# Layer B of a two-layer decoder: the next group's decay rows, key products and first base steps are made in slots 9 to 15 of the running group

## The reference

```python
conv = silu(causal_conv4(proj));  q, k, v = split(conv)
q = l2norm(q) * SCALE;  k = l2norm(k)
beta = sigmoid(b);  g = -exp(a_log) * softplus(a + dt_bias);  gc = cumsum(g in the chunk)
decay = exp(gc_i - gc_j) for j <= i
lmat = strict_lower(beta * k k^T * decay)
u, w = solve (I + lmat) [v*beta | k*beta*exp(gc)]
aqk = (q k^T) * decay;  kdec = k * exp(g_last - gc)
per chunk: v_new = u - w S;  o = (q exp(gc)) S + aqk v_new;  S = S exp(g_last) + kdec^T v_new
```

## Time and profile before

| what | value |
|---|---|
| median of 3 runs | 2171.14 us (2170.03 to 2179.94) |
| the profiled execution, its own time | 2173.54 us |
| its span, first to last instruction | 2171.6 us |
| mean granted TensorE clock over the span | 0.989 of full |
| busy: PE, DVE, ACT, POOL | 97%, 45%, 32%, 21% |
| layer B's group rounds | about 1117 to 1733 us of the span |

### The profile page before, as it was taken

The page is one execution under the profiler, slowest core; times in us unless marked ns, Lnnn a source line. Parts: engine busy times, 40 slices in busy tenths (PEclk is TensorE's granted clock), DMA queues, the critical chain, the costliest instruction groups (busy, mean ns, idle before and its releaser), DMA issues.

```text
span 2171.6 us, 39599 instructions
## 1 busy us (share of the span) xinstructions
PE 2110.4 (97%) x16046; PEld 1508.9 (69%) x16046; DVE 986.9 (45%) x2521; ACT 688.4 (32%) x1615; POOL 450.8 (21%) x640
## 2 busy tenths in 40 slices
PE   8999999999999999999999999999998999999998
PEld 6888888888888876554566666666666666665444
DVE  5244354354344444321256666666666233333252
ACT  4122321312222131311145454444544344542101
POOL 0512231242124205000033312332231200020000
PEclk9999999999999999999999999999998999999999
DMA  7412201212221156777012212221110262124451
GB/s 234 151 41 67 81 26 46 78 40 56 74 59 42 30 183 226 228 220 219 23 57 92 75 74 86 74 85 76 59 42 13 62 269 82 39 74 140 135 167 53
DMA packets 210250, 210.53 MB, mean 97 GB/s; under 512 B 14262, under 2 KB 181654, under 8 KB 209151
## 3 DMA queue, kind: packets, MB, share of 16 engines
q1 hardware_dynamic: 198070, 148.27, 23.0%
q0 software_dynamic: 12000, 59.73, 7.1%
HBM read 179.56 MB, written 68.23 MB: 114 GB/s over the span
## 4 chain that ended last, share of the span: by engine, by line
PE 47%; DVE 3%; ACT 1%; issue 0%; DVEq 0%
PE bank L2093 17%; PE bank L2857 8%; PE bank L3347 7%; PE bank L2151 4%; PE bank L2167 2%; PE bank L2149 2%; DVE arena L2591 1%; PE bank L2159 1%; PE bank L2873 1%; PE bank L2882 1%; PE bank L3325 1%; PE bank L3358 0%; PE bank L2182 0%; PE bank L3254 0%; PE bank L3231 0%; ACT L2354 0%
## 5 line engine op out<-in xcount | busy, mean ns | idle before, releaser
L887 PE MATMUL bank<-arena 128*128 128x256 f32 (+1 forms) x2688 | 631.7, 386 | 0.0
L887 PEld LDWEIGHTS bank<-arena 128*128 128x128 f32 x2688 | 494.5, 190 | 75.3
L2093 PE MATMUL bank<-arena 128*128 128x352 f32 x1296 | 462.9, 474 | 0.1
L2093 PEld LDWEIGHTS bank<-arena 128*128 128x128 f32 x1296 | 219.8, 193 | 65.3 <-issue 0.6
L2857 PE MATMUL bank<-arena 128*128 128x352 f32 x576 | 176.4, 459 | 0.0
L3347 PE MATMUL bank<-arena 128*128 128x512 f32 x360 | 167.5, 599 | 0.0
L2151 PEld LDWEIGHTS bank<-arena 128*128 128x128 f32 x864 | 128.8, 196 | 42.9 <-DVE arena L2605 5.0
L2857 PEld LDWEIGHTS bank<-arena 128*128 128x128 f32 x576 | 106.6, 190 | 53.3
L2151 PE MATMUL bank<-arena 128*128 128x128 f32 x864 | 133.9, 282 | 3.8 <-DVE arena L2605 3.8
L1341 POOL TENSOR_TENSOR arena<-arena 128x272 f32<-128x272 f32 (+1 forms) x48 | 31.5, 656 | 507.9 <-ACT arena L1061 488.0
L1323 POOL TENSOR_TENSOR arena<-arena 128x512 f32<-128x512 f32 x96 | 122.7, 1278 | 10.9 <-POOL arena L1323 0.9
(11 more groups left out here) (430 smaller groups left out, 2783.7 us busy)
## 6 DMA issues: line engine op xcount, KB each, us to landing
arena<-in_w_in_a SPq DMA_DIRECT2D x48, 512.0 KB, 5.2
arena<-in_w_in_b SPq DMA_DIRECT2D x40, 512.0 KB, 5.1
arena<-in_cache_win_k SPq DMA_DIRECT2D x48, 256.0 KB, 6.2
arena<-in_cache_win_v SPq DMA_DIRECT2D x48, 256.0 KB, 4.7
out<-arena SPq DMA_DIRECT2D x40, 256.0 KB, 3.4
arena<-in_w_mem_kv SPq DMA_DIRECT2D x16, 512.0 KB, 8.1
arena<-in_cache_mem_k SPq DMA_DIRECT2D x32, 256.0 KB, 4.6
arena<-in_cache_mem_v SPq DMA_DIRECT2D x32, 256.0 KB, 3.8
```

The source lines that it names most:

```text
L887: m = nc.tensor.matmul(o[:, 0:hi - lo], w, y, start=k == 0 and i in (0, 1, 3, 5), stop=k == KH - 1, skip_group_check=i in (2, 4, 6))
L2093: m = nc.tensor.matmul(bank[j % 3][:, 0:PART], ring.slots[:, (B1 + b) % RING, k, :], part_in(k, part_), start=k == 0, stop=k == KD - 1)
```

## The change

Rows rl, their exponentials, kk, the choice of 8x8 blocks, the base rows and the first two base steps of group G+1 are made in slots 9 to 15 of round G, into a second buffer (`LTs`). ra and qk of group G move to slots 9 and 11, kt to 6, vt to 15. The levels move to slots 4 to 7, 10 and 12 to 14: level 5's z from slot 13 to 12, level 6's x from 14 to 13, level 3's x from 6 to 4. The exponentials of ra(G) and rl(G+1) come together in ACT's slot 9. The convolution, tap and SiLU tables change; SiLU 0 of group G+2 moves from slot 7 to slot 12, SiLU 1 from 12 to 13, SiLU 2 from 15 to slot 0 of the next round. The output turn moves from slot 9 to 8. The base steps leave out column 0 of their chosen blocks, which no step reads. Ahead of the loop rl, kk and two base steps of group 0 are made. The diff, cut to its core:

```diff
-    picked = upper[:, 0:P].rearrange("p (c j b) -> p c j b", j=BASE, b=NBASE)
+    picked = upper[:, 0:4 * (BASE - 1) * NBASE].rearrange("p (c j b) -> p c j b", c=4, b=NBASE)
-    spread_rows = upper[:, 2176:2176 + 4 * BASE * 32]
+    spread_rows = upper[:, 2176:2176 + 4 * (BASE - 1) * 32]
+    LTs = [LT, upper[:, 3072:3584].rearrange("p (c e) -> p c e", e=P)]
...
-    PREP = {0: ("rl", "ra"), 1: ("kk", "qk"), 10: ("kt",), 11: ("vt",)}
-    LEVEL_SLOTS = {(3, "x"): 6, (3, "z"): 7, (4, "x"): 8, (4, "z"): 9, (5, "x"): 12, (5, "z"): 13, (6, "x"): 14, (6, "z"): 15}
-    BASE_STEPS = {2: 2, 3: 2, 4: 2, 5: 1}
-    BASE_END = max(BASE_STEPS)
-    AT_SS, AT_ROOTS, AT_INV, AT_LOGS, AT_FACTORS, AT_OT = 3, 4, 5, 6, 7, 9
+    PREP = {6: ("kt",), 9: ("ra", "rl"), 11: ("qk", "kk"), 15: ("vt",)}
+    NEXT = ("rl", "kk")
+    LEVEL_SLOTS = {(3, "x"): 4, (3, "z"): 5, (4, "x"): 6, (4, "z"): 7, (5, "x"): 10, (5, "z"): 12, (6, "x"): 13, (6, "z"): 14}
+    AT_ROWS = 13
+    STEPS_BEFORE = {14: 1, 15: 1}
+    STEPS = {0: 1, 1: 2, 2: 1, 3: 1}
+    EARLY_STEPS = sum(STEPS_BEFORE.values())
+    AT_EXPS = 9
+    AT_SS, AT_ROOTS, AT_INV, AT_LOGS, AT_FACTORS, AT_OT = 3, 4, 5, 6, 7, 8
-    def p_names(s):
-        return PREP.get(s, ()) + ((level_name(*level_in[s]),) if s in level_in else ())
+    def p_names(G, s):
+        names = [(G + (n in NEXT), n) for n in PREP.get(s, ())]
+        if s in level_in:
+            names.append((G, level_name(*level_in[s])))
+        return [(g, n) for g, n in names if g < NG_]
...
-    work = [(0, "ss")]
+    work = [(0, "ss"), (0, "rl"), (0, "kk")]
-                work += [(G, n) for n in p_names(s)]
+                work += p_names(G, s)
...
-    TAP_AT = {3: 0, 8: 1, 11: 2}
-    conv_at = {4: (0, 1), 5: (0, 2), 7: (0, 3), 9: (1, 1), 11: (1, 2), 12: (1, 3), 13: (2, 1), 14: (2, 2), 15: (2, 3)}
-    silu_at = {7: 0, 12: 1, 15: 2}
+    TAP_AT = {0: 0, 4: 1, 11: 2}
+    conv_at = {1: (0, 1), 3: (0, 2), 4: (0, 3), 5: (1, 1), 7: (1, 2), 8: (1, 3), 12: (2, 1), 14: (2, 2), 15: (2, 3)}
+    silu_at = {12: 0, 13: 1}
...
-                if c:
-                    readout(pe, g, f"ks{c}")
+                readout(pe, g, f"ks{c}" if c else "vt")
-        def matrix_step(G, s):
+        def turned(G, name):
-            if s == 0:
+            if name == "rl":
+            elif name == "ra":
-            elif s == 1:
+            elif name == "kk":
+            elif name == "qk":
-            if "kt" in PREP.get(s, ()):
+            elif name == "kt":
-            if "vt" in PREP.get(s, ()):
+            elif name == "vt":
+        def matrix_step(G, s):
+            cs, lt = range(*GR[G % 2]), LTs[G % 2]
+            for g, name in p_names(G, s):
+                if name in PREP.get(s, ()):
+                    turned(g, name)
...
-                        to_blocks(G, f"x{k}", [(i, 16 * n, LT[q, n, q], side(Md[q, n, :], k, 0))
+                        to_blocks(G, f"x{k}", [(i, 16 * n, lt[q, n, q], side(Md[q, n, :], k, 0))
...
-        for u in units[NORM_AT:PER_HEAD + AHEAD]:
+        for u in units[NORM_AT:PER_HEAD + KD]:
+            unit(*u)
+        turned(0, "rl")
+        for u in units[PER_HEAD + KD:PER_HEAD + 2 * KD]:
+            unit(*u)
+        turned(0, "kk")
+        for u in units[PER_HEAD + 2 * KD:PER_HEAD + AHEAD]:
...
-        for i in range(3):
-            silu(1, i)
-        for u in ended(units[PER_HEAD:PER_HEAD + AHEAD]):
-            piece(*u)
+        first, second, third = ended(units[PER_HEAD:PER_HEAD + AHEAD])
+        piece(*first)
+        silu(1, 0)
+        exps(0, "rl", LT, 0)
+        piece(*second)
+        silu(1, 1)
+        silu(1, 2)
+        piece(*third)
-                    if s == 0:
-                        exps(G, "rl", LT, 0)
-                    elif s == 1:
+                    if s == AT_EXPS:
+                        if G + 1 < NG_:
+                            exps(G + 1, "rl", LTs[(G + 1) % 2], 0)
...
+                if 0 < G < NG_ - 1 and s == 0:
+                    silu(G + 1, 2)
...
             nc.vector.tensor_scalar(brT[:, g // 2, g % 2 * 512:(g % 2 + 1) * 512], b[:, :], onw, None,
                                     ALU.mult).then_inc(rd_dve, 1)
+        def turned(G, name):
+
+            h, cs = group(G)
+            lt, factors_of = LTs[G % 2], hd[:, h % 2]
+            b = left(dve, G, name)
+            if name == "rl":
+                nc.vector.tensor_tensor(lt, bk(b), wide4(mat(M_GT)), ALU.add).then_inc(rd_dve, 1)
+            elif name == "ra":
+                nc.vector.tensor_tensor(AT[:, cs, :], bk(b), wide4(mat(M_GE)), ALU.add).then_inc(rd_dve, 1)
+            elif name == "kk":
+                dve.wait_ge(exd, 2 * G + 1)
+                nc.vector.tensor_tensor(lt, lt, bk(b), ALU.mult).then_inc(rd_dve, 1)
+            elif name == "qk":
+                dve.wait_ge(exd, 2 * G + 2)
+                nc.vector.tensor_tensor(AT[:, cs, :], AT[:, cs, :], bk(b), ALU.mult).then_inc(rd_dve, 1)
+            elif name == "kt":
+                dve.wait_ge(hdv, 3 * G + 3)
+                nc.vector.tensor_tensor(kdec[:, cs, :], bk(b), factors_of[:, KD_, cs].unsqueeze(2)
+                                        .to_broadcast([P, 4, P]), ALU.mult).then_inc(rd_dve, 1)
+            elif name == "vt":
+                nc.vector.tensor_tensor(vb[:, cs, :], bk(b), hcols(beta, h)[:, cs].unsqueeze(2)
+                                        .to_broadcast([P, 4, P]), ALU.mult).then_inc(rd_dve, 1)
+
+        def choose_blocks(G):
+
+            readout(dve, G, "kk")
+            for i in range(4):
+                q = quarter(i)
+                nc.vector.tensor_tensor(picked[q].rearrange("p c j b -> p c b j"),
+                                        LTs[G % 2][q, :, q].rearrange("p c (b j) -> p c b j", j=BASE)[:, :, :, 1:],
+                                        mats[q, M_HSEL, 4:4 + NBASE].unsqueeze(1).unsqueeze(3)
+                                        .to_broadcast([32, 4, NBASE, BASE - 1]), ALU.mult).then_inc(base, 1)
+
         def matrix_step(G, s):
             h, cs = group(G)
...
+            for g, name in p_names(G, s):
                 if name in PREP.get(s, ()):
...
+                    turned(g, name)
             if s in level_in:
                 k, x = level_in[s]
                 hi = P // 2
...
-                                .to_broadcast([P, 4 * BASE, NBASE, BASE])).then_inc(base, 1)
+                                .to_broadcast([P, 4 * (BASE - 1), NBASE, BASE])).then_inc(base, 1)
-            rows_ = spread_rows.rearrange("p (c j b e) -> p c j b e", c=4, j=BASE, b=NBASE)[:, :, j, :, 0:j]
+            rows_ = spread_rows.rearrange("p (c j b e) -> p c j b e", c=4, b=NBASE, e=BASE)[:, :, j - 1, :, 0:j]
...
+                readout(dve, g, "vt")
...
-        for g in range(2):
-            for i in range(3):
-                for w in range(CW):
-                    conv(g, i, w)
-                if (g, i) == (0, 0):
-                    gate_sums_read()
-                if (g, i) == (0, 2):
-                    norm_inverses(0)
+        for i in range(3):
+            for w in range(CW):
+                conv(0, i, w)
+            if not i:
+                gate_sums_read()
+        norm_inverses(0)
+        for w in range(CW):
+            conv(1, 0, w)
+        turned(0, "rl")
+        for w in range(CW):
+            conv(1, 1, w)
+        turned(0, "kk")
+        choose_blocks(0)
+        for w in range(CW):
+            conv(1, 2, w)
+        base_rows(0)
+        for n in range(EARLY_STEPS):
+            base_step(0, n)
...
-                if G < NG_ and s in BASE_STEPS:
-                    before = sum(n for t, n in BASE_STEPS.items() if t < s)
-                    if not before:
-                        base_rows(G)
-                    for n in range(before, before + BASE_STEPS[s]):
+                if G < NG_ and s in STEPS:
+                    first = EARLY_STEPS + sum(n for t, n in STEPS.items() if t < s)
+                    for n in range(first, first + STEPS[s]):
-                    if s == BASE_END:
+                    if first + STEPS[s] == BASE - 1:
+                if G + 1 < NG_:
+                    if s == AT_ROWS - 2:
+                        choose_blocks(G + 1)
+                    elif s == AT_ROWS:
+                        base_rows(G + 1)
+                    elif s in STEPS_BEFORE:
+                        first = sum(n for t, n in STEPS_BEFORE.items() if t < s)
+                        for n in range(first, first + STEPS_BEFORE[s]):
+                            base_step(G + 1, n)
```

More of the change, by code:

```diff
@@ L2231, in matrix_step @@
                     if k < LEVELS - 2:
-                        to_blocks(G, f"x{k}", [(i, 16 * n, LT[q, n, q], side(Md[q, n, :], k, 0))
+                        to_blocks(G, f"x{k}", [(i, 16 * n, lt[q, n, q], side(Md[q, n, :], k, 0))
                                                for n, i, q, _ in over])
                     elif k < LEVELS - 1:
```

(28 more changed lines are left out.)

## The result

The changed kernel takes 2255.16 us in the median of 4 runs (2251.71 to 2260.40), the kernel before 2171.72 us in the same comparison. The ratio is 1.0378, 95% interval 1.0345 to 1.0412: slower by 3.8%, where 4.4% was forecast, and 13 us under the predicted time. The profiled execution took 2254.04 us, its span is 2252.1.

The account below looks back on a forecast made before the run. PE, busy 97%, was taken as the bound. From 2173.5 us profiled, -24.4 - 4.8 - 15.3 + 79 + 3 + 44 + 13.6 + 1.4 gave 2270.0; less 2.4 to the median, 2268 us, range 2205 to 2310.

Parts of the forecast that it names:

- Base steps ahead: PE's wait for the block transpose before level 3 goes, -24.4 us; other waits from the same crowded slots go, -4.8 us.
- POOL's queue: Late SiLU delays POOL's squares and spread; PE waits 6.1 us at level 6's x, +79 us; round 0 adds 3.
- The table load: On ACT ahead of slot 12's SiLU: 1.28 us by the trace, without the skill page's further 1.38 us drain.
- the rival with a longer switch: ACT drains longer ahead of the SiLU, each wait about 1.28 us longer: 17 us more, 2285 us; chance 0.04.
- Clock: PE's clock loss behind old waits goes, -15.3 us; half clock behind each new wait costs 3.4 us, +44 us.
- Exponentials together: In ACT's slot 9 eight exponentials delay vn's copy; PE waits 0.8 us in 12 rounds, 2 in two: +13.6 us.
- Ahead of the loop: PE's turn of rl(0) waits for DVE's convolution (1, 0), small head terms and factors: +1.4 us.
- The rival on the other side: POOL's spread is in time, so level 6's x doesn't wait and the gain stands: 2142 us; chance 0.08.

Follow-up runs that it names:

- The repaired kernel: The changed kernel with POOL's spread ahead of squares(G+2, 0) and, on ACT, rl(G+1)'s exponentials behind vn's copy: 2145.65 us, ratio 0.9866.
- two moves in the old order: The kernel before with base steps and transpose ahead of DVE's factor work, and convolution steps (0, 1) and (0, 2) one slot later: 2147.76 us, ratio 0.9870.
- the kernel with the steps first: The kernel before with DVE's base steps and block transpose ahead of out_factors, norm_inverses and factors in each slot: 2155.64 us, ratio 0.9905.
- squares twice: The changed kernel with squares(G+2, 0) made twice on POOL, one more operation ahead of the spread: 2281.27 us, ratio 1.0492.

## Why the prediction was right

By its own steps, in its order:

- **Base steps ahead**, -24.4 and -4.8 us: the first is exact, since no wait for the transpose is left. Of the 4.8 us, 1.4 are left for r_sb. The reason given, crowded slots, was not the right one: a change of order in the same slots took 17.7 of the 24.4 us.
- **POOL's queue**, +79 and +3 us: the mechanism is as put, link by link. Counted from PE's start of slot 12 at 1445.76, the copy of qs ends at +2.1 (forecast +2.1), the SiLU at +4.2 (+4.0), the spread at +6.9 (+7.3), DVE's reading at +7.9 (+8.2), and PE starts at +8.0 (+8.3). In a round PE stands 5.7 us and not 6.1. The term that was too large is the spread: 1.63 us for the 2.17 of the earlier trace rows, a round in which POOL's first operation started behind a convolution step of DVE; in nine of the 16 rounds of before the two took 1.7. In round 0 PE's wait is 2.05 us for 3, and in round 13 it is 6.3.
- **The table load**: 1.28 us with the SiLU's first operation 0.01 us behind it, as the earlier trace rows had it, so the rival with a longer switch falls. The 1.38 us of drain that the Trainium skill gives, ScalarE: Activation LUTs, section What ACT_TABLE_LOAD costs, are not in this trace.
- **Clock**: -15.3 and +44, so +28.7 us of PE's time. This is the term that was mis-sized most. In the group rounds the kernel before lost 16.6 us and the changed one 31.9, of which 4.6 in the last rounds and 27.2 around the waits of rounds 1 to 12; over the whole span the difference is 11.7. That the clock falls at each of these waits was right. The step that failed is the price of one, 3.4 us, taken as the middle of two losses and kept though the wait is longer than those before: it is 2.3, because the spell at 1.2 GHz begins while PE still stands.
- **Exponentials together**, +13.6 us: 9.9. In the steady round PE waits 0.4 us and not 0.8; once the long wait was gone, the total was 15.6.
- **Ahead of the loop**, +1.4: 1.2 us.

By the profiled executions the forecast was +96.5 us and the span grew by 80.5, 16 us less. The errors of the terms are -5.2 (82 forecast and 76.8 found for the wait at level 6), -17.0 (clock), -3.7 (vn), -0.2 (ahead of the loop) and +1.4 (r_sb); against them stand the 7.2 us of PE's busy time that are not clock and that no term of the sum had. That is -17.5 in all. So the mechanism was right, and the sum is as near as it is in part by luck: without the 7.2 us it would have been 7 us further off. The ends of the range were not added up rightly either: its own terms give 2196 for the lower (2268 - 44 - 14 - 13.6) and about 2300 for the upper, not 2205 and 2310. The result lies well inside both.

The rival on the other side, a spread in time, had its condition right: once it was in time, the kernel was faster than before, though by 0.5% and not by the 1.4% that it gave. In the profiled executions the gain was 13.0 us and not 29.5. The rival had taken the other waits and the lost clock as gone; the rows show 3.6 us left at level 6's x, 2.7 for r_sb, 2.0 more than its 13.6 for vn, and PE's busy time shorter by 9.3 us and not 15.3. The repaired kernel's 0.9866 is what the rival gave, but by luck: it has hardly a wait for vn, which the rival had counted.

Two things the prediction did not see. It took the change's gain as one that needed the change, where two moves in the old order give the same. And it called the slots of the base steps crowded, where the trace of before already held the better reason: a last step that stood behind work waiting for ACT and also ran at a fifth of its speed.

## What to carry to other kernels

When work moves between slots, look for the engine whose program was not edited: its order still holds the old promise, here that a SiLU comes six slots before its round's spread is wanted. Follow each moved result to everything that waits in the same queue behind its reader, not only to the reader. And before building a second buffer to take work off a path, read the timeline of the last microseconds ahead of the wait: a wait for another engine, or an operation five times its usual length, may be moved away by a change of order alone, as it was here.

## What the runs showed of the hardware

**DVE beside POOL.** In the kernel before, DVE's L2591 with 16 columns took 0.97 us, until POOL's scaling L2761 was over:

```profile
1311.49 1.03 POOL L2761 TENSOR_TENSOR arena<-arena 128x512 f32<-128x512 f32 x1 [3.68 <-DVE arena L2503]
1311.60 0.97 DVE L2591 TENSOR_TENSOR arena<-arena 128x16 f32<-128x16 f32 x1
```

The first ends at 1312.52, the second at 1312.57. The same pair stands in 14 of the 16 rounds, and the step takes 0.96 to 1.03 us in each. In the kernel with the steps first it took 0.19 us in all 16, with no scaling of POOL beside it. It goes the other way too: where POOL's first spread operation starts just behind a convolution step of DVE (L2458), as in the round of the earlier trace rows (1321.51 behind 1321.44) and three others, it takes 1.13 to 1.15 us and not 0.62. The Trainium skill, SBUF — State Buffer, section Who interferes with whom, says that a DVE instruction with two SBUF inputs contends with a GpSimd instruction that reads SBUF. The trace agrees: in these rows the one that starts later is the one that is lengthened, and it ends only after the earlier one has ended.

**A longer wait can cost less clock.** The half-clock spells around the waits at level 6's x, in rounds 1 to 12 of each kernel: waits of 1.2 to 1.3 us (SiLU in slot 10) had none of their own; 3.6 to 3.7 us (late SiLUs in the kernel before) cost 2.9 us each, with a spell of 6.8 us in nine rounds and of 3.4 in three; 5.6 to 5.8 us (the changed kernel) cost 2.3, with 6.8 in all twelve; and 6.7 to 7.0 us (squares twice) cost 2.8, with 6.8 in six and 10.2 in six. What PE loses is only the part of a spell in which it has work, so where the spell lies against the end of the wait counts as much as how long the wait is. The rest of each round differs between these kernels as well, and that was not held apart.
